# Low parts of the w_in tiles on GpSimd in a two-layer hybrid decoder step

## The reference: what is computed

```python
h = rmsnorm(x, g_pre)
(c_x, c_b, c_c, c_z, g_q, g_k, g_v, g_lr, g_z,
 s_q, s_k, s_v, s_z, m_q, m_z) = split_cols(h @ w_in)
cy, new_conv = short_conv(c_c * c_x, conv_buf, conv_w)              # A
a_out = c_b * cy * jax.nn.silu(c_z)
o_b, new_gla = gla_recurrence(...)                                  # B, 4 heads of 64
o_c, new_k, new_v = swa_sink_attention(q_c, k_c, s_v, ...)          # C, window 128
o_d = memory_attention(m_q, mem_k, mem_v)                           # D, 256 memory tokens
mix = jnp.concatenate([a_out, b_out, c_out, d_out], axis=-1) @ w_out
y = x + rmsnorm(mix, g_post)
```

## Time and profile before

| | |
|---|---|
| median of 3 runs | 2256.68 us (2256.25 to 2257.54) |
| the profiled execution, its own time | 2257.99 us |
| its span on the core | 2256.2 us |
| granted TensorE clock, mean | 0.997 of full speed |
| busy PE, DVE, ACT, POOL | 2217.0, 1309.3, 896.1, 104.9 us |

### The profile page before, as it was taken

One profiled execution on the slowest core, in us unless ns is written; L12 is line 12 of the kernel. 1 busy time (PEld: TensorE's weight loads), 2 busy tenths in 40 slices (PEclk: granted clock), 3 DMA queues, 4 the chain that ended last, 5 costly groups with the idle time before them and its releaser, 6 DMA issues. The chain is left out here.

```text
span 2256.2 us, 39965 instructions
## 1 busy us (share of the span) xinstructions
PE 2217.0 (98%) x14924; PEld 1805.2 (80%) x14924; DVE 1309.3 (58%) x2870; ACT 896.1 (40%) x2015; POOL 104.9 (5%) x179
## 2 busy tenths in 40 slices
PE   8999999999999999999999999999999999999998
PEld 4778877778788888878877878777878988887887
DVE  4467755565376755646535776556645676654542
ACT  4444233344354333434425442244435442343421
POOL 1000000000000000000000000000100000000000
PEclk9999999999999999999999999999999999999999
DMA  7111212244211122324331121232441113141322
GB/s 245 38 57 29 58 37 66 66 141 145 85 39 30 43 64 74 71 77 141 132 91 41 29 52 43 52 99 82 142 132 45 39 30 77 35 106 40 100 103 75
DMA packets 230554, 172.12 MB, mean 76 GB/s; under 512 B 56886, under 2 KB 206908, under 8 KB 230332
## 3 DMA queue, kind: packets, MB, share of 16 engines
q1 hardware_dynamic: 226100, 154.78, 24.4%
q10 hardware_dynamic: 4264, 14.78, 1.9%
HBM read 136.60 MB, written 21.93 MB: 70 GB/s over the span
## 5 line engine op out<-in xcount | busy, mean ns | idle before, releaser
L1767 PE MATMUL bank<-h_hi,w_hi 128*128 128x512 f32 (+3 forms) x2160 | 482.1, 361 | 14.8 <-issue 5.2
L1767 PE MATMUL bank<-h_lo,w_hi 128*128 128x512 f32 (+3 forms) x2160 | 484.5, 361 | 2.0
L1767 PE MATMUL bank<-h_hi,w_lo 128*128 128x512 f32 (+2 forms) x2080 | 461.6, 360 | 2.0
L1767 PEld LDWEIGHTS bank<-h_hi,w_hi 128*128 128x128 f32 (+1 forms) x2160 | 353.0, 185 | 90.0 <-issue 31.5
L1767 PEld LDWEIGHTS bank<-h_lo,w_hi 128*128 128x128 f32 (+1 forms) x2160 | 353.4, 185 | 73.1 <-issue 13.6
L1767 PEld LDWEIGHTS bank<-h_hi,w_lo 128*128 128x128 f32 x2080 | 344.2, 188 | 65.8 <-issue 14.1
L2813 PE MATMUL bank<-scr_r,tb_r 128*128 128x512 f32 x816 | 195.1, 396 | 1.0 <-issue 1.0
L2813 PEld LDWEIGHTS bank<-scr_r,tb_r 128*128 128x128 f32 x816 | 151.7, 188 | 35.7 <-issue 2.3
L2138 ACT ACTIVATE tb<-bank 128x512 f32<-128x512 f32 (+1 forms) x140 | 71.3, 509 | 218.0 <-PE bank L1767 207.8
L2294 ACT ACTIVATE scr<-bank 128x1024 f32<-128x1024 f32 x64 | 65.7, 1027 | 194.7 <-PE bank L2045 194.7
L2875 ACT ACTIVATE junk<-bank 128x512 bf16<-128x512 f32 x68 | 40.6, 597 | 240.9 <-PE bank L2813 231.2
(11 more groups left out here) (297 smaller groups left out, 2911.6 us busy)
## 6 DMA issues: line engine op xcount, KB each, us to landing
w_raw<-in_w_in SPq DMA_DIRECT2D x96, 512.0 KB, 3.8
out<-scr SPq DMA_DIRECT2D x32, 512.0 KB, 2.7
scr<-in_w_out SPq DMA_DIRECT2D x16, 512.0 KB, 5.2
w_raw<-in_w_out SPq DMA_DIRECT2D x16, 512.0 KB, 3.8
scr<-in_x_prompt SPq DMA_DIRECT2D x16, 512.0 KB, 3.6
scr<-out SPq DMA_DIRECT2D x16, 512.0 KB, 3.3
rot<-out ACTq DMA_DIRECT2D x12, 512.0 KB, 3.6
mix_t<-in_x_prompt ACTq DMA_DIRECT2D x8, 512.0 KB, 13.8
```

The lines of the kernel that those rows point to most:

```text
L1767: m = mm(bank[b][0:m_w, 0:c1 - c0], w[:, slot, k, 0:m_w], h[:, k, c0:c1], start=it["piece"] == 0 and k == 0, stop=it["piece"] == 2 and k = ...
```

## The change

The subtraction that makes `w_lo` moves from DVE to POOL, and the planner books it there, at 2.4 us in place of 1.15, so that the list of items is another one too.

```diff
@@ Forecast.place
         elif k == "wlow":
             if not it["ready"]:
-                at[("lo", it["tile"])] = run("DVE", 1.15, when(("hi", it["tile"])))
+                at[("lo", it["tile"])] = run("POOL", 2.4, when(("hi", it["tile"])))
@@ follow
-        while lows and lows[0][0] <= max(fc.t["PE"], fc.t["DVE"]):
+        while lows and lows[0][0] <= max(fc.t["PE"], fc.t["POOL"]):
             wlow()
@@ on_vector
-                if kind == "wlow":
-                    t = it["tile"]
-                    if t < RING:
-                        continue
-
-                    dve.wait_ge(w_hi_done, t + 1)
-                    n, i = split_width(t), t % RING
-                    tt(lo_of(t), w_raw[:, i, :, 0:n], w_hi[:, i, :, 0:n].bitcast(F32), ALU.subtract).then_inc(w_lo_done, 1)
-                elif kind == "conv_in":
+                if kind == "conv_in":
@@ on_gpsimd
+                elif kind == "wlow":
+                    t = it["tile"]
+                    if t < RING:
+                        continue
+
+                    pool.wait_ge(w_hi_done, t + 1)
+                    n, i = split_width(t), t % RING
+                    tt(lo_of(t), w_raw[:, i, :, 0:n], w_hi[:, i, :, 0:n].bitcast(F32), ALU.subtract).then_inc(w_lo_done, 1)
```

## The result

The changed kernel takes 2330.57 us (median of 4 runs, 2324.5 to 2334.02) against 2256.61 us before (4 runs as well): a ratio of 1.0323, 95% interval [1.031, 1.0335]. It is slower by 74 us. The profiled execution has a span of 2332.2 us. The prediction said 2255.7 us, at most 2267, and gave "slower" 0.25.

What follows compares the result with a forecast made beforehand. PE, busy 98% of the span with unchanged work, was taken to bound the kernel. Terms -2 - 2 + 0 + 3 = -1 us gave 2255.7 us by the median, range 2246 to 2267.

Steps and rivals of the forecast that it cites:

- slower: Whole kernel: the outcome that the change measurably lengthens the time, given chance 0.25.
- step 1: DVE: 92 subtractions leave, so PE waits less for DVE; -2 us, ends 0 and -4.2.
- Step 2: PE: 12 fewer returns to the projection, so fewer changes of matmul kind; -2 us, gains from 0 to 9.2.
- the 4.2 us of waits: PE's waits for DVE inside the passes that a relieved DVE could give back, out of 8.2 us.
- some of these small waits will be made again elsewhere: DVE's new order fills the freed time, so only half of the 4.2 us was taken as gain.
- Step 3: POOL: one subtraction takes 2.0 us, 1.1 to 4 allowed; w_lo still reaches PE in time, cost 0.
- Step 4: DVE beside POOL's subtraction: 32 instructions held 45 us together, partly reaching PE; +3 us, ends 0 and 22.
- the 5.6 us behind it: Turns on PE: 32 holds, a quarter coming through at 0.7 us, if all stood before something PE needs.
- lock rival: Passes: POOL's subtraction holds the shared port, so DVE makes turns or banks late; 2264 to 2274.7 us, chance 0.23.
- the 4.0 us: Two PE waits of 2.0 us at the second passes' ends, behind an `out` split; would stay unchanged.
- PE's waits for DVE grow beyond 20 us: Sign in the profile after that the prediction is wrong; waits of 5 to 12 us were expected.

Runs made afterwards that it cites:

- order_alone: Kernel before with the changed kernel's list of items, subtraction still on VectorE: 2318.65 us, ratio 1.0272.
- scale_first: list_sample with the scale of C1's last score moved ahead of the sample score's maximum on VectorE, once per layer: 2296.83 us.
- engine_eight: engine_alone with each subtraction split into eight pieces of 128 columns: 2265.54 us, ratio 1.0041.
- engine_alone: Kernel before with its old list of items, subtraction moved to GpSimd: 2281.76 us, ratio 1.0104.
- write_beside: Kernel before, subtraction on VectorE, plus ten idle chained fills of 64 columns on GpSimd after high parts: 2257.1 us, ratio 0.9999.
- read_beside: Kernel before, subtraction on VectorE, plus seven idle chained two-input subtractions of 64 columns on GpSimd after high parts: 2261.45 us, ratio 1.002.
- engine_two: engine_alone with each subtraction split into two pieces of 512 columns: 2278.14 us, ratio 1.0089.
- list_sample: Kernel before, subtraction on VectorE, with the changed kernel's list only in the two passes with the sample: 2312.46 us, ratio 1.0246.

## Why the prediction was wrong

**The step that failed is 2, with step 1.** Step 2 costed a reordered list by its changes of kind on PE: "12 x 0.16 = 1.9 us", with ends of 0 and 9.2 us, all of them gains. Step 1 gave the new list, at the worst, 0 of the 4.2 us of waits back. Measured: the list alone costs 61 us (order_alone). Both steps looked at what the order before had left to gain, and neither costed what a new order can break: VectorE works off its items in the order of the list, so one that waits for a DMA ahead of a gate stalls TensorE for 4.8 us. The gain that step 2 did cost isn't there either: the weight loads' "issue" time before projections went up from 59.2 to 71.1 us where 57 was forecast, and without the two gates of 5.0 us each that stand in it it is 61. The text did say "some of these small waits will be made again elsewhere". In the change they were made again, with 40.0 us in place of 8.2. That reordering could lose was in no rival, and so none had the measured size.

**A multiplier was missing.** No step had the clock in it. The stalls of 3 us at one place in each layer came with the lower level, and taking them out gave back 5.7 us of idle and 12.3 us of busy time (scale_first). Of the 76 us of span, 30 are busy time, most or all of it clock.

**Step 3 was right.** One subtraction takes 2.40 us (median; 2.0 taken, 1.1 to 4 allowed), and no wait of TensorE names GpSimd; engine_eight, with the latest low parts, is the fastest of the three. The estimate of 2.3 us from the Trainium skill, GPSIMD Engine Reference, "Elementwise — side-by-side cycle accounting", was nearer than mine: the two inputs are not read as fast as the copies suggest. GpSimd was busy 326.0 us, where 290 was forecast.

**Step 4 had the right mechanism and the wrong size.** The term was +3 us, ends 0 and 22; engine_alone gives 24.4. I expected 32 holds and 45 us; in engine_alone there were 52 and 76.2 us. Of the 52, eight are copies (12.3 us), which my count had left out, and eight are masked copies, 0.15 us each, which may be noise; the other 36 were held 1.7 us each in place of 1.4. Of the holds 32% came through, where my +3 us of 45 is 7% and the 5.6 us behind it 12.5%. Even the lock rival, 2264 to 2274.7 us, was below the 2281.8 of engine_alone. That VectorE waits for the whole instruction was cited from the Trainium skill, SBUF — State Buffer, "Who interferes with whom"; the trace agrees (97.95 above). VectorE's busy time was forecast near 1200 us and is 1283.5, by these holds.

**Step 1, the 4.0 us** at the end of the second passes were there unchanged, as said. The text's own test, "PE's waits for DVE grow beyond 20 us", is met at 40.0.

What stays open: 25 us of the list's 56 in the sample passes, for which the third place and the clock behind it are the likely home, not shown by a run; why order and engine together cost less than their sum; and whether another setting of the planner would beat the list of before. No kernel here does.

## What to carry to other kernels

When a planner's cost changes, the whole list is new. Time the new list with the old engines first, and the old list with the new engine; here these two kernels would have told nearly all. To see how much a list owes to luck, change a number of its planner by a few per cent, up and down, and time what comes out. Where the bound engine is 98% busy, price an edit by what it can break: look for queue items that wait for something slow ahead of one that frees the bound engine, and count a stall of some 3 us at twice or more its length if the clock falls behind it (here 6 us of stalls gave back 15.6).

## What the runs showed of the hardware

- VectorE's tiniest instructions in SBUF (128x4, one input) are held by a two-input instruction on GpSimd, from 0.17 to 1.51 us (engine_alone and the change). Fills of 64 columns on GpSimd held none beyond 0.16 us (write_beside).
- GpSimd's two-input subtraction takes 0.29 us for 64 columns (median of 644, read_beside), 1.29 for 512 (median of 184, engine_two) and 2.40 for 1024 (median of 92, the change): (2.40 - 0.29) / 960 = 2.2 ns for each column.
- TensorE's granted clock fell to its lower level in the middle of a kernel in which it was busy 97% (list_sample), around a stall of 2.99 us; the same eight matmuls of 512 columns took 3.75 us in place of 2.10. Behind a wait of 2.0 us it fell in one layer of the kernel before (2143 us) and not in the other (1042 us).
